# Gate and up products from the residual before its norm, the norm's root multiplied into their results

## The reference, cut to what matters

```python
def rmsnorm(x, g):
    y = xf * lax.rsqrt(jnp.mean(xf * xf, axis=-1, keepdims=True) + RMS_EPS)
    return (y * g.astype(jnp.float32)).astype(x.dtype)
...
        x = x + rmsnorm(mix, attn_post_g[i])
        h = rmsnorm(x, mlp_pre_g[i])
        gu = h @ w_gate_up[i].astype(h.dtype)
        a, u = jnp.split(gu, [D_FF], axis=-1)
        a = causal_dwconv(a, conv_w[i], conv_b[i])
        y = (jax.nn.gelu(a, approximate=True) * u) @ w_down[i].astype(h.dtype)
        x = x + rmsnorm(y, mlp_post_g[i])
```

## Time and profile before

| | |
|---|---|
| median of 3 runs | 1874.45 us (1870.66 to 1877.84) |
| profiled execution | 1875.21 us, span 1873.4 us |
| mean granted TensorE clock | 0.925 |
| TensorE busy | 1614.9 us, 86% |
| VectorE busy | 931.8 us, 50% |
| ScalarE busy | 453.1 us, 24% |
| GpSimd busy | 751.8 us, 40% |

### The profile page before, as it was taken

The page is one execution under the profiler, slowest core; times in us unless marked ns, Lnnn a source line. Parts: engine busy times, 40 slices in busy tenths (PEclk is TensorE's granted clock), DMA queues, the critical chain, the costliest instruction groups (busy, mean ns, idle before and its releaser), DMA issues.

```text
span 1873.4 us, 26208 instructions
## 1 busy us (share of the span) xinstructions
PE 1614.9 (86%) x9902; PEld 1348.6 (72%) x9902; DVE 931.8 (50%) x1903; ACT 453.1 (24%) x1098; POOL 751.8 (40%) x452
## 2 busy tenths in 40 slices
PE   6989889599999899597977777999979877789999
PEld 4766447288888677476976666779979865667799
DVE  6535660656666200434665475736236675765161
ACT  3335562312222100212121122331021122232210
POOL 4422204156666455253432332324535322333364
PEclk8989889799999899798987888999989887889999
DMA  5210001122223222121211111112212111111122
GB/s 205 68 45 28 8 1 57 34 79 93 97 90 101 68 90 90 56 79 56 74 57 34 46 46 45 48 56 67 83 57 70 57 45 46 35 45 57 49 90 99
DMA packets 35491, 119.53 MB, mean 64 GB/s; under 512 B 5056, under 2 KB 5696, under 8 KB 35136
## 3 DMA queue, kind: packets, MB, share of 16 engines
q1 hardware_dynamic: 34096, 115.73, 18.7%
q10 hardware_dynamic: 1296, 2.40, 0.4%
HBM read 116.02 MB, written 2.10 MB: 63 GB/s over the span
## 4 chain that ended last, share of the span: by engine, by line
PE 77%; DVE 15%; ACT 5%; issue 2%; POOL 0%; DMA 0%; DVEq 0%; POOLq 0%; ACTq 0%
PE ps L524 63%; PE ps L537 3%; PE ps L879 2%; PE ps L671 2%; PE ps L925 2%; PE ps L544 2%; DVE score L1765 2%; PE ps L605 2%; DVE score L1764 2%; DVE score L1752 1%; DVE tmp L1391 1%; ACT probs L1314 1%; PE ps L538 1%; PE ps L802 1%; ACT probs L1105 1%
## 5 line engine op out<-in xcount | busy, mean ns | idle before, releaser
L524 PE MATMUL ps<-hh,whi 128*128 128x264 f32 (+3 forms) x2056 | 682.8, 332 | 148.6 <-DVE merge L1725 53.2
L524 PE MATMUL ps<-hl,whi 128*128 128x264 f32 (+3 forms) x2056 | 668.0, 325 | 0.0
L524 PE MATMUL ps<-hh,wlo 128*128 128x264 f32 (+3 forms) x2056 | 666.0, 324 | 0.0
L477 POOL TENSOR_SCALAR whi<-raw 128x1024 fp32r<-128x1024 f32 x192 | 207.5, 1081 | 914.0 <-PE ps L524 914.0
L524 PEld LDWEIGHTS ps<-hh,whi 128*128 128x128 f32 (+1 forms) x2056 | 407.3, 198 | 202.0 <-issue 113.1
L480 POOL TENSOR_TENSOR wlo<-raw,whi 128x1024 fp32r<-128x1024 f32 x192 | 469.9, 2447 | 16.0
L524 PEld LDWEIGHTS ps<-hl,whi 128*128 128x128 f32 (+1 forms) x2056 | 407.0, 198 | 26.9 <-issue 1.4
L524 PEld LDWEIGHTS ps<-hh,wlo 128*128 128x128 f32 (+1 forms) x2056 | 406.9, 198 | 25.3
L1378 DVE RECIPROCAL rstd<-rstd 128x512 f32<-128x512 f32 x4 | 13.4, 3353 | 203.3 <-ACT rstd L1021 203.3
L537 PE MATMUL ps<-const,probs 128*128 128x128 f32 x360 | 68.4, 316 | 22.3 <-ACT pts L1330 15.2
L1783 DVE CUSTOM_DVE_ANT_0 probs<-ps,keep 128x144 f32<-128x144 f32 (+4 forms) x72 | 31.0, 467 | 111.3 <-PE ps L879 110.9
(11 more groups left out here) (266 smaller groups left out, 2224.9 us busy)
## 6 DMA issues: line engine op xcount, KB each, us to landing
raw<-in_w SPq DMA_DIRECT2D x208, 512.0 KB, 3.4
x<-in_x SPq DMA_DIRECT2D x4, 512.0 KB, 7.4
out<-x SPq DMA_DIRECT2D x8, 256.0 KB, 4.5
cw_k<-in_cw1k SPq DMA_DIRECT2D x1, 1024.0 KB, 5.3
cw_v<-in_cw1v SPq DMA_DIRECT2D x1, 1024.0 KB, 7.3
const<-in_const ACTq DMA_DIRECT2D x1, 528.0 KB, 8.6
pT<-in_p ACTq DMA_DIRECT2D x1, 512.0 KB, 3.6
poolw<-in_poolw ACTq DMA_DIRECT2D x2, 256.0 KB, 3.7
```

Of the source, the lines that this page charges most:

```text
L477: pool.tensor_scalar(whi[s][:], raw[s][:], 1.0, 0.0, ALU.mult, ALU.add)\
L524: mm = pe.matmul(out, lhs, rhs, start=start and n == 0, stop=stop and n == 2)
```

## The change

The root of the second norm is one number for a position, and the products sum over channels. So the kernel now feeds the products `x` times the channel's weight, and VectorE multiplies both results of each item with `rstd`. The high and low parts are made inside the loop that updates the residual: ScalarE's copy with the channel weight as its scale, VectorE's `mpre_low` for the chunk before. TensorE makes the first item's two units side by side, chunk by chunk, and adds the sum of squares of the chunk behind its six products. In each item VectorE first writes `up` and `gate`, PSUM times `rstd`, into `tmp`; the convolution and the last multiplication read these.

```diff
--- before.py
+++ after.py
@@ -706,16 +706,15 @@
                 if m:
                     sum_squares("post", [X[:, 0, :]], lambda k: [tmp[:, k % 2, 0:S]], [m - 1])
             sum_squares("post", [X[:, 0, :]], lambda k: [tmp[:, k % 2, 0:S]], [DC - 1])
-            sum_squares("mpre", [X[:, 1, :]], lambda k: [tmp[:, k % 2, 0:S]])
-
-
-            pe.wait_ge(*at("h_low", ("mpre", DC - 1)))
+
 
             def gate_up(i, first):
                 for pair in range(2):
                     if not first:
 
                         pe.wait_ge(ty.sem("act_low"), 2 * i + pair - 1)
+                    if first and pair == 0:
+                        continue
                     for j in range(2):
                         pe.wait_ge(ty.sem("unit_split"), 4 * i + (U_GU + 2 * pair + j + 1))
                         for k in range(DC):
@@ -723,6 +722,16 @@
                                        hh[:, k, 0:S], hl[:, k, 0:S], k == 0, k == DC - 1)
                         mm.then_inc(ty.sem("unit_used"), 1)
 
+            for j in range(2):
+                pe.wait_ge(ty.sem("unit_split"), U_GU + j + 1)
+            for k in range(DC):
+                pe.wait_ge(*at("h_low", ("mpre", k)))
+                for j in range(2):
+                    mm = three(G[:, j, :], whi[j][:, k], wlo[j][:, k], hh[:, k, 0:S], hl[:, k, 0:S],
+                               k == 0, k == DC - 1)
+                    if k == DC - 1:
+                        mm.then_inc(ty.sem("unit_used"), 1)
+                sum_squares("mpre", [X[:, 1, :]], lambda k: [tmp[:, k % 2, 0:S]], [k])
             gate_up(0, True)
             with pe.Fori(1, FC // 2) as i:
                 gate_up(i, False)
@@ -1139,10 +1148,12 @@
                     act.wait_ge(*at("squares_summed", ("post", m - 2)))
                 act.activation(tmp[:, m % 2, 0:S], y(m), ACT.Square).then_inc(*tick("squared", ("post", m)))
             root("post", rstd[:, 0:S], X[:, 0, :], 1.0 / D)
-            square_all("mpre", lambda k: x[:, k, META:T], lambda k: at("x_new", ("post", k)),
-                       lambda k: tmp[:, k % 2, 0:S])
+            for k in range(DC):
+                act.wait_ge(*at("x_new", ("post", k)))
+                act.activation(hh[:, k, 0:S], x[:, k, META:T], ACT.Copy, scale=vec[:, V_MPRE + k:V_MPRE + k + 1])\
+                    .then_inc(*tick("h_high", ("mpre", k)))
+                square("mpre", k, x[:, k, META:T], at("x_new", ("post", k)), tmp[:, k % 2, 0:S])
             root("mpre", rstd[:, 0:S], X[:, 1, :], 1.0 / D)
-            high_parts("mpre", lambda k: tmp[:, 2 + k % 2, 0:S], lambda k: hh[:, k, 0:S])
 
 
             def gate_up(i):
@@ -1372,7 +1383,7 @@
 
         @block.vector
         def _(dve):
-            def norm(tag, src, normed, cols, gain, r, out=None):
+            def norm(tag, src, normed, cols, gain, r, out=None, then=None):
 
                 dve.wait_ge(*at("rms", tag))
                 dve.reciprocal(r, r).then_inc(*tick("rstd", tag))
@@ -1397,8 +1408,12 @@
                         dve.wait_ge(*at("normed", (tag, k)))
                         xs = x[:, k, cols]
                         dve.tensor_tensor(xs, xs, normed(k), ALU.add).then_inc(*tick("x_new", (tag, k)))
+                        if then and k:
+                            then(k - 1)
                 if out:
                     low(DC - 1)
+                elif then:
+                    then(DC - 1)
 
             def vcol(v0):
                 return lambda k: vec[:, v0 + k:v0 + k + 1]
@@ -1563,9 +1578,16 @@
             def y(m):
                 return probs[:, m // 4, m % 4, 0:S]
 
-            norm("post", y, lambda k: tmp[:, 2 + k % 2, 0:S], seq, vcol(V_POST), rstd[:, 0:S])
-            norm("mpre", lambda k: x[:, k, seq], lambda k: tmp[:, 2 + k % 2, 0:S], seq, vcol(V_MPRE),
-                 rstd[:, 0:S], (lambda k: hh[:, k, 0:S], lambda k: hl[:, k, 0:S]))
+            def mpre_low(k):
+                dve.wait_ge(*at("h_high", ("mpre", k)))
+                dve.scalar_tensor_tensor(out=hl[:, k, 0:S], in0=x[:, k, seq], scalar=vcol(V_MPRE)(k),
+                                         in1=hh[:, k, 0:S].bitcast(F32), op0=ALU.mult, op1=ALU.subtract)\
+                    .then_inc(*tick("h_low", ("mpre", k)))
+
+            norm("post", y, lambda k: tmp[:, 2 + k % 2, 0:S], seq, vcol(V_POST), rstd[:, 0:S], then=mpre_low)
+            dve.wait_ge(*at("rms", "mpre"))
+            dve.reciprocal(rstd[:, 0:S], rstd[:, 0:S]).then_inc(*tick("rstd", "mpre"))
+            dve.wait_ge(*at("rstd", "mpre"))
 
 
             def gate_up(i):
@@ -1574,28 +1596,32 @@
                     ps = (G, S0)[pair]
                     conv, work, inner, full_ = (probs[:, pair, s, 0:S] for s in range(4))
 
+                    gate, up = tmp[:, pair, 0:S], tmp[:, 2 + pair, 0:S]
+
                     def step(ins, k):
                         ins.then_inc(ty.sem("conv_step"), 1)
-                        dve.wait_ge(ty.sem("conv_step"), 4 * n + k)
+                        dve.wait_ge(ty.sem("conv_step"), 5 * n + k)
 
                     def cw(k):
                         return vec[:, V_CONVW + k * FC:V_CONVW + (k + 1) * FC][:, bass.ds(n, 1)]
 
                     dve.wait_ge(ty.sem("unit_used"), 4 * i + (U_GU + 2 * pair + 2))
-                    step(dve.tensor_scalar(conv, ps[:, 0, :], cw(2), vec[:, V_CONVB:V_CONVB + FC][:, bass.ds(n, 1)],
-                                           ALU.mult, ALU.add), 1)
-                    step(dve.scalar_tensor_tensor(out=conv[:, 1:S], in0=ps[:, 0, 0:S - 1], scalar=cw(1),
-                                                  in1=conv[:, 1:S], op0=ALU.mult, op1=ALU.add), 2)
-                    dve.scalar_tensor_tensor(out=conv[:, 2:S], in0=ps[:, 0, 0:S - 2], scalar=cw(0),
+                    dve.tensor_tensor(up, ps[:, 1, :], rstd[:, 0:S], ALU.mult)
+                    step(dve.tensor_tensor(gate, ps[:, 0, :], rstd[:, 0:S], ALU.mult), 1)
+                    step(dve.tensor_scalar(conv, gate, cw(2), vec[:, V_CONVB:V_CONVB + FC][:, bass.ds(n, 1)],
+                                           ALU.mult, ALU.add), 2)
+                    step(dve.scalar_tensor_tensor(out=conv[:, 1:S], in0=gate[:, 0:S - 1], scalar=cw(1),
+                                                  in1=conv[:, 1:S], op0=ALU.mult, op1=ALU.add), 3)
+                    dve.scalar_tensor_tensor(out=conv[:, 2:S], in0=gate[:, 0:S - 2], scalar=cw(0),
                                              in1=conv[:, 2:S], op0=ALU.mult, op1=ALU.add)\
                         .then_inc(ty.sem("conv_done"), 1)
                     dve.wait_ge(ty.sem("conv_squared"), n + 1)
-                    step(dve.tensor_scalar(inner, work, GELU_B, 1.0, ALU.mult, ALU.add), 3)
+                    step(dve.tensor_scalar(inner, work, GELU_B, 1.0, ALU.mult, ALU.add), 4)
                     dve.tensor_tensor(inner, inner, conv, ALU.mult).then_inc(ty.sem("act_in"), 1)
                     dve.wait_ge(ty.sem("act_tanh"), n + 1)
                     step(dve.scalar_tensor_tensor(out=inner, in0=work, scalar=1.0, in1=conv,
-                                                  op0=ALU.add, op1=ALU.mult), 4)
-                    dve.scalar_tensor_tensor(out=full_, in0=inner, scalar=0.5, in1=ps[:, 1, :],
+                                                  op0=ALU.add, op1=ALU.mult), 5)
+                    dve.scalar_tensor_tensor(out=full_, in0=inner, scalar=0.5, in1=up,
                                              op0=ALU.mult, op1=ALU.mult).then_inc(ty.sem("act_full"), 1)
                     dve.wait_ge(ty.sem("act_high"), n + 1)
                     dve.tensor_tensor(actl[:, n, :], full_, acth[:, n, :].bitcast(F32), ALU.subtract)\
```

## The result

The changed kernel takes 1934.37 us (median of 4 runs, 1930.51 to 1936.08), the one before 1876.14 (4 runs): a ratio of 1.031, 95% interval 1.028 to 1.033. The forecast was 1899, the range 1879 to 1912. The direction was right, the loss of 58.2 us is 2.4 times the 24.4 that I had summed.

The account below looks back on a forecast made before the run. TensorE set the loop's pace before; after the change VectorE, held by GpSimd's splits, would. Item 0 from 371.4 and the items end the loop at 651.1 instead of 626.7: +24.4 us, forecast 1899, range 1879 to 1912.

Parts of the forecast that it names:

- The norm: At the second norm: overlapping products with the residual loop starts item 0 at 371.4 instead of 385.0, gaining 13.6 us.
- the late split: After the first pair of weight units: GpSimd splits the next unit only then, so TensorE idles 2.7 us, covered.
- The new work: In each loop item: VectorE's work without holds rises from 8.2 to 9.5 us, alone fitting under TensorE's 11.12.
- The holds: In the loop: GpSimd's splits, 6.9 us per item, can hold eight of VectorE's ten instructions, before four of eight.
- What follows the loop: Down product and other layers: untouched, moving with the loop's end, forecast 24.4 us later.
- the mean item: In the loop: VectorE sets the pace at 12.9 us per item; means of 12.3 and 13.4 give the range.
- the sum: Over the loop: item 0 takes 11.8 us, 20 items at 12.9 take 258, the last takes 9.9; end at 651.1.
- the ring: In the loop: TensorE's 11.12, L477's 1.06, L1601's 0.55 and waits of 0.05 set equal items of 12.8 us.
- the clock: In the loop: TensorE's pauses of 1 to 2 us were taken as too short for the clock to fall; chance 0.06.
- The signs: In the later profile: VectorE still waiting before each item, unheld `tmp` steps, or loop clock well under 1 would refute it.
- My walk: Through loop items: two hold patterns, 12.1 and 14.0 us, alternate, 13.05 us on the mean.
- the clock falls every item: Rival, in the loop: a falling clock makes items up to 14 us, +46.5 us, time 1922; chance 0.06.

Follow-up runs that it names:

- the short split: Changed kernel with GpSimd's subtraction L480 working on one chunk of eight in the loop, the other low weights left as they were; 1865.43 us, ratio 0.995.
- last_psum: Changed kernel, but the `up` product is written back in place into PSUM, while `gate` still goes through `tmp`; 1934.68 us, ratio 1.033.
- early_release: Changed kernel, but TensorE waits only until item n - 2 is copied out of PSUM, not until its `actl` is made; 1909.64 us, ratio 1.019.
- loop_only: Norm of the kernel before with the loop of the changed kernel, so the root is multiplied in twice; 1951.39 us, ratio 1.041.
- up_in_wait: Changed kernel with the product for `up` moved behind the third convolution step, into VectorE's wait for ScalarE's square; 1934.59 us, ratio 1.032.
- conv_psum: Changed kernel, but the `gate` product is written back in place into PSUM, while `up` still goes through `tmp`; 1890.39 us, ratio 1.009.

## Why the prediction was right in direction and wrong in size

**Right.** *The norm.* Item 0 at VectorE at 371.4, found 370.84; a gain of 13.6 us, found 13.4 in the trace and 13.9 in the time of the norm alone. Chunks of 2.25 us, a root at 367.2, an idle TensorE of 2.7 us for the late split: found 2.25, 366.54 and 2.25. *The new work* is 9.5 us an item and would hide under TensorE's 11.12: the short split shows it, 11.12 us per item. *The holds* of GpSimd's splits on the steps that read `tmp` are the cause: shown from two sides, by the shorter split and by PSUM in place of `tmp`. *What follows the loop* moves with it: +58.3 us at its end, +58.2 in the time.

**Wrong: one term, the mean item, "I take 12.9"; measured 14.51.** From item 0 to the last the sum had 11.8 + 258 = 269.8 us, and the trace has 304.70: item 0 took 2.0 us more than its 11.8, and the 20 others 14.55 on the mean, 33 us more. Less 1.1 us at the two ends, this is the 33.8 us that 24.4 lacks of 58.2. Two steps stand behind it, the ring and the clock. The signs that I had named for being wrong came in part: VectorE waits for TensorE before every second item, and the granted clock in the loop is 0.91.

*The ring.* I wrote it as TensorE's 11.12, "L477's 1.06 behind its second unit", and 0.55. That supposed that VectorE's last steps get in between L477 and L480. In the trace they don't. The chain begins at the first step: L1611 is held to 518.35, and so L1620 asks at 521.50, 0.23 us after an L480 has begun, and is held to 524.27. From there L1627 can't ask before 527.31, an estimate from the rows' durations (525.70 + 0.69 + 0.92) with L1624 not held, and the next L480 has begun at 526.78. That L1624 asks 0.05 us after L477 and is held too makes it 528.15, but decides nothing: in `last_psum` L1624 is free and L1627 still meets the split. My walk had the first half of this, the item whose first step and whose L1593 and L1594 are held, 14.0 us; it lacked the holds on the last two steps (0.84 and 1.14 us), with which the item takes 15.64. What the ring holds is the whole split: 0.23 to L477, 1.04, 0.09, 2.65, then 0.55 and 0.13 to TensorE, together the 4.69 us of its pause. So TensorE doesn't pause "1 to 2 us" in each item, but 4.69 in every second. The items don't become equal, as I had supposed: the pause leaves GpSimd idle, the item that runs then is held nowhere, or only at its last step, ends early, and lets TensorE run on for the item that is held. With the clock always up, a pair would take 22.5 + 4.69 = 27.2 us, 13.6 per item. That is 0.7 over my 12.9, an estimate of 14 us over the loop.

*The clock.* I gave 0.06 to a clock that falls in every item, against it that the pauses were shorter than the 2 to 4 us after which it had fallen. The pause was not short: in the 3 us after it the granted clock is 0.52. Nor was shortness a safe argument, since in `early_release` three of twelve waits of some 2.06 us had half clock behind them. The rest, 14.55 - 13.6 = 0.95 us per item or 19 us over the loop, is the clock's: it is what TensorE's ten stretches of 96 products are longer than at full clock. Unused products that keep the clock up give back 15.5 us, with holds that fall otherwise. Both parts are shown; that they are 14 and 19 us rests on the estimate of 22.5 us for a stretch at full clock.

The rival "the clock falls every item" came near in time (1922) with too low a chance. In mechanism it is half right: every second item, and behind a pause more than twice as long as its text had.

**Open.** The distance behind the unheld item is 13.0 and 14.0 us in turn (up to 14.5 at the start) in the changed kernel, `loop_only` and `up_in_wait`. It goes with the clock: behind the pause that ends at 501.55 the products are back at full pace 2.9 us later and the stretch takes 23.87 us, behind the one that ends at 530.11 it is 5.1 us later and 24.84. The granted clock over the pause itself was 0.95 in the first case and 0.82 in the second, so it had fallen earlier there. Why it falls now earlier and now later no run shows. That `last_psum` gains nothing, while `conv_psum` gains 44 us, fits the chain above: only with the gate in PSUM is the first step free, and then L1620 is through (515.76 in the item shown) before its L480 begins (517.24).
